# The second and third norm of a transformer step: rows scaled and transposed in place of a product with a diagonal, and half a unit started early

## The reference

```python
def rms_norm(x, w):
    xf = x.astype(jnp.float32)
    y = xf * lax.rsqrt(jnp.mean(xf * xf, axis=-1, keepdims=True) + NORM_EPS)
    return (y * w.astype(jnp.float32)).astype(x.dtype)

def modulate(h, shift, scale):
    return h * (1 + scale) + shift

def ffn_sublayer(x, shift, scale, gate, norm_w, wi, wo):
    return x + 0.5 * gate * swiglu(modulate(rms_norm(x, norm_w), shift, scale), wi, wo)

def mixer_inputs(x, shift, scale, norm_w, w_in):
    z = modulate(rms_norm(x, norm_w), shift, scale) @ w_in
    ...
```

## Time and profile before

| | us |
|---|---|
| median of three runs | 2199.97 (2198.9 to 2200.54) |
| the profiled execution | 2200.38 |
| its span, from first to last instruction | 2198.3 |
| TensorE busy in it | 2168.2 |
| VectorE busy | 1658.8 |
| ScalarE busy | 1077.2 |

### The profile page before, as it was taken

One profiled execution on the slowest core, in us unless ns is written; L12 is line 12 of the kernel. 1 busy time (PEld: TensorE's weight loads), 2 busy tenths in 40 slices (PEclk: granted clock), 3 DMA queues, 4 the chain that ended last, 5 costly groups with the idle time before them and its releaser, 6 DMA issues.

```text
span 2198.3 us, 28344 instructions
## 1 busy us (share of the span) xinstructions
PE 2168.2 (99%) x10272; PEld 1734.6 (79%) x10272; DVE 1658.8 (75%) x1903; ACT 1077.2 (49%) x1450; POOL 65.3 (3%) x55
## 2 busy tenths in 40 slices
PE   6999999999999999999999999999999999999999
PEld 3567777777777778888888888888888888888887
DVE  3447888888888889756867888885578686776856
ACT  3335444545435446455545545465554455555453
POOL 0001000000000000001600000100000000000000
PEclk9999999999999999999999999999999999999999
DMA  9998888888888876555536776845665757557573
GB/s 367 386 379 302 295 317 315 281 303 286 316 308 289 290 262 221 184 173 172 187 109 233 258 254 236 292 161 207 235 235 192 267 191 267 191 202 257 190 233 131
DMA packets 273333, 548.14 MB, mean 249 GB/s; under 512 B 9014, under 2 KB 9418, under 8 KB 273008
## 3 DMA queue, kind: packets, MB, share of 16 engines
q1 hardware_dynamic: 212676, 423.69, 55.7%
q10 hardware_dynamic: 57484, 113.47, 14.3%
q0 software_dynamic: 3104, 10.05, 1.6%
HBM read 543.71 MB, written 3.46 MB: 249 GB/s over the span
## 4 chain that ended last, share of the span: by engine, by line
PE 95%; DVE 2%; DMA 1%; ACT 1%; issue 0%; SPq 0%; ACTq 0%; DVEq 0%
PE ps L714 30%; PE ps L716 29%; PE ps L715 29%; PE ps L655 1%; PE ps L640 1%; DMA ada_w_sb<-in_ada_w 1%; DVE w_lo L1833 1%; PE ps L701 0%; PE ps L1091 0%; PE ps L1159 0%; PE ps L1167 0%; DVE xm L1953 0%; ACT w_hi L1342 0%; DVE vec_acc L1893 0%; DVE scan L2272 0%
## 5 line engine op out<-in xcount | busy, mean ns | idle before, releaser
L1342 ACT CAST w_hi<-raw_w 128x1024 fp32r<-128x1024 f32 x728 | 765.0, 1053 | 991.8 <-PE ps L716 942.5
L1833 DVE TENSOR_TENSOR w_lo<-raw_w,w_hi 128x1024 fp32r<-128x1024 f32 x728 | 896.4, 1235 | 384.7 <-ACT w_hi L1342 381.8
L714 PE MATMUL ps<-w_hi,xT_hi 128*128 128x512 f32 x2080 | 821.0, 395 | 5.5 <-DVE xT_lo L1921 4.2
L716 PE MATMUL ps<-w_hi,xT_lo 128*128 128x512 f32 x2080 | 810.7, 390 | 0.0
L715 PE MATMUL ps<-w_lo,xT_hi 128*128 128x512 f32 x2080 | 810.6, 390 | 0.0
L714 PEld LDWEIGHTS ps<-w_hi,xT_hi 128*128 128x128 f32 x2080 | 391.0, 188 | 110.2 <-issue 24.5
L716 PEld LDWEIGHTS ps<-w_hi,xT_lo 128*128 128x128 f32 x2080 | 390.8, 188 | 82.7
L715 PEld LDWEIGHTS ps<-w_lo,xT_hi 128*128 128x128 f32 x2080 | 391.0, 188 | 78.6
L1893 DVE SCALAR_TENSOR_TENSOR vec_acc<-ada_w_sb,ctile,vec_acc 128x512 f32<-128x512 f32 x420 | 299.2, 746 | 0.0
L714 PE MATMUL ps<-w_hi,hT_hi 128*128 128x512 f32 x704 | 275.8, 392 | 0.0
L716 PE MATMUL ps<-w_hi,hT_lo 128*128 128x512 f32 x704 | 274.1, 389 | 0.0
(11 more groups left out here) (287 smaller groups left out, 1059.2 us busy)
## 6 DMA issues: line engine op xcount, KB each, us to landing
raw_w<-in_ffn_wi SPq DMA_DIRECT2D x176, 1024.0 KB, 4.9
ada_w_sb<-in_ada_w ACTq DMA_DIRECT2D x96, 1024.0 KB, 8.0
raw_w<-in_ffn_wo SPq DMA_DIRECT2D x88, 1024.0 KB, 5.2
raw_w<-in_w_in SPq DMA_DIRECT2D x68, 1024.0 KB, 5.2
ada_w_sb<-in_ada_w SPq DMA_DIRECT2D x30, 1024.0 KB, 12.8
raw_w<-in_w_out SPq DMA_DIRECT2D x16, 1024.0 KB, 5.2
ada_m<-in_ada_w ACTq DMA_DIRECT2D x12, 1024.0 KB, 6.8
raw_w<-in_w_proj_m SPq DMA_DIRECT2D x8, 1024.0 KB, 5.1
```

What stands on the lines that cost most here:

```text
L714: pe.matmul(out, a_hi, w_hi[:, slot, kk, :], start=(first and kk == 0), stop=False)
L716: mm = pe.matmul(out, a_lo, w_hi[:, slot, kk, :], start=False, stop=(last and kk == 1))
L1342: act.copy(w_hi[:, us % SPL, :, :], raw_w[:, slot, 2 * half:2 * half + 2, :]).then_inc(hi_ready, 1)
L1833: dve.tensor_tensor(w_lo[:, us % SPL, :, :], raw_w[:, slot, 2 * half:2 * half + 2, :], w_hi[:, us % SPL, :, :].bitcast(F32), ALU.subtract) ...
```

## The change

In the second and third norm the diagonal goes. VectorE scales quarters 0 and 2 of a group's row by the inverse root and ScalarE quarters 1 and 3, into `acc` (second norm) or the new `rows_out` (third norm), and TensorE transposes the 16 blocks with the identity. The PSUM banks are laid out anew, four tiles to a bank. ScalarE now takes the even pairs and VectorE the odd ones. The context's part of pair 0 is cast and subtracted by itself, and TensorE runs the context's half of unit 0 ahead of the sample's transposes; the sample's half follows them. On VectorE the split of unit 1 moves ahead of the context's last two pairs, the half subtraction for the context stands ahead of the sample's inverse, and the splits of units 2 and 3 follow the subtractions of pairs 1 and 3. On ScalarE the splits ahead of the third norm are two in place of three; the third follows the cast of pair 1. For the second norm the sample's square of quarter 2 is taken after both context squares. The first norm keeps its diagonal.

```diff
-            def norm(s):
-
-                for g in range(GROUPS):
-                    pe.wait_ge(diag_ready, 2 * s + g + 1)
-                    for j in range(8):
...
-                        for b in range(2):
-                            k = 2 * j + b
-                            mm = pe.matmul(ps[:, j, b * TOK + g * P:b * TOK + (g + 1) * P],
-                                           x[:, g, k * P:(k + 1) * P], diag[:, g, :], start=True, stop=True)
-                        mm.then_inc(norm_ps, 1)
+            def norm_T(s, g, i):
+
+                pe.wait_ge(scaled_dve, 4 * (s - 1) + 2 * g + i // 2 + 1)
+                pe.wait_ge(scaled_act, 4 * (s - 1) + 2 * g + i // 2 + 1)
+                if g == LAT and i == 2:
+                    pe.wait_ge(xm_act, modulated(s, 2, CTX))
+                if g == LAT and i == 3:
+                    pe.wait_ge(xm_ready, modulated(s, 3, CTX))
+                for k in [2 * j + b for j in range(8) if norm_bank(j) == i for b in range(2)]:
+                    mm = pe.transpose(norm_tile(s, g, k), scaled_rows[s][:, g, k * P:(k + 1) * P], ident)
+                mm.then_inc(norm_ps, 1)
+
+            def norm_chunk(s, us):
+
+                for i in range(4):
+                    norm_T(s, CTX, i)
+                pe.wait_ge(xT_lo_ready, lows_before(s) + 1)
+                unit(us, 0, xT_hi, xT_lo, 0, 0, True, False, groups=(CTX,))
+                for i in range(4):
+                    norm_T(s, LAT, i)
+                for k in range(8):
+                    pe.wait_ge(xT_lo_ready, lows_before(s) + k + 2)
+                    unit(us + k, 0, xT_hi, xT_lo, 2 * k, 0, k == 0, k == 7, groups=(LAT,) if k == 0 else (CTX, LAT))
...
+            def scaled(s, g, n):
+
+                act.wait_ge(inverse_ready, 2 * s + g + 1)
+                c = slice(n * CH, (n + 1) * CH)
+                act.activation(scaled_rows[s][:, g, c], x[:, g, c], ACT.Copy, scale=small[:, 14 + g:15 + g]).then_inc(scaled_act, 1)
...
                 act.wait_ge(acol_ready, s + 4)
-                modulate(1, CTX)
+                modulate(0, CTX)
                 act.wait_ge(x_updated, s * NCH)
                 sumsq(s, 3, LAT)
+                hi(0, (CTX,))
                 root(s, LAT)
-                modulate(3, CTX)
-                modulate(5, CTX)
-                modulate(7, CTX)
-                modulate(1, LAT)
-                hi(0, 5)
-                hi(1, 5)
-                if s == 1:
-                    split(u0 + 2, 0)
-                modulate(3, LAT)
-                hi(2, 6)
-                hi(3, 6)
-                modulate(5, LAT)
-                hi(4, 7)
-                hi(5, 7)
+                modulate(2, CTX)
+                scaled(s, LAT, 1)
+                scaled(s, LAT, 3)
+                modulate(4, CTX)
+                modulate(6, CTX)
+                modulate(0, LAT)
+                hi(0, (LAT,))
+                hi(1)
+                split(u0 + 2, 0)
+                modulate(2, LAT)
+                hi(2)
+                hi(3)
                 split(u0 + AHEAD, 0)
-                modulate(7, LAT)
-                hi(6, 8)
-                hi(7, 8)
+                modulate(4, LAT)
+                hi(4)
+                hi(5)
+                modulate(6, LAT)
+                hi(6)
+                hi(7)
...
-                    for g in range(GROUPS):
-                        sumsq(1, 2, g)
+                    sumsq(1, 2, CTX)
                     act.wait_ge(x_ctx, 1)
                     sumsq(1, 3, CTX)
+                    sumsq(1, 2, LAT)
                     root(1, CTX)
+                    scaled(1, CTX, 1)
+                    scaled(1, CTX, 3)
                     split(U_IN + 1, 0)
...
-            for n in range(AHEAD):
-                split(U_F2 + n, 0)
+            split(U_F2, 0)
+            act.wait_ge(mac_done, VEC_F2)
+            scaled(2, CTX, 1)
+            scaled(2, CTX, 3)
+            split(U_F2 + 1, 0)
...
+            def scaled(s, g, n):
+
+                dve.wait_ge(inverse_ready, 2 * s + g + 1)
+                c = slice(n * CH, (n + 1) * CH)
+                dve.tensor_scalar(scaled_rows[s][:, g, c], x[:, g, c], small[:, 14 + g:15 + g], None, ALU.mult).then_inc(scaled_dve, 1)
...
                 dve.wait_ge(acol_ready, s + 4)
-                modulate(0, CTX)
+                modulate(1, CTX)
                 variance(s, LAT, 2 * NCH)
-                diagonal(s, LAT)
-                modulate(2, CTX)
-                modulate(4, CTX)
-                modulate(6, CTX)
-                modulate(0, LAT)
-                modulate(2, LAT)
-                lows(0, 1)
+                low_of(1, 0, (CTX,))
+                inverse(s, LAT)
+                scaled(s, LAT, 0)
+                scaled(s, LAT, 2)
+                modulate(3, CTX)
                 split(u0 + 1, 0)
-                modulate(4, LAT)
-                lows(2, 3)
+                modulate(5, CTX)
+                modulate(7, CTX)
+                modulate(1, LAT)
+                low_of(2, 0, (LAT,))
+                low_of(3, 1)
                 split(u0 + 2, 0)
-                modulate(6, LAT)
-                lows(4, 5)
+                modulate(3, LAT)
+                low_of(4, 2)
+                low_of(5, 3)
                 split(u0 + 3, 0)
-                lows(6, 7)
+                modulate(5, LAT)
+                low_of(6, 4)
+                low_of(7, 5)
+                modulate(7, LAT)
+                low_of(8, 6)
+                low_of(9, 7)
...
-                        variance(1, CTX, 2 * NCH - 1)
-                        diagonal(1, CTX)
+                        variance(1, CTX, 2 * NCH - 2)
+                        inverse(1, CTX)
+                        scaled(1, CTX, 0)
+                        scaled(1, CTX, 2)
...
             variance(2, CTX, 2 * NCH - 1)
-            diagonal(2, CTX)
+            inverse(2, CTX)
+            scaled(2, CTX, 0)
+            scaled(2, CTX, 2)
             split(U_F2, 0)
             dve.wait_ge(units_done, U_F2)
-            dve.tensor_tensor(y_tmp[:, LAT, :], ps[:, 3, :], gate_bc[:, LAT, c], ALU.mult).then_inc(y_read, 1)
-            dve.wait_ge(y_read, 1)
+            chain(dve.tensor_tensor(y_tmp[:, LAT, :], ps[:, 3, :], gate_bc[:, LAT, c], ALU.mult))
             dve.tensor_tensor(x[:, LAT, c], x[:, LAT, c], y_tmp[:, LAT, :], ALU.add).then_inc(x_updated, 1)
```

More of the change, by code:

```diff
@@ L276, in build @@
         hcT_lo = place("hcT_lo", [P, KD, TOK], F32R)
+        rows_out = place("rows_out", [P, GROUPS, D], at=SCR)
+        top[0] = SCR + (W_AT - SCR) % 256 + 32768
         vec_o = place("vec_o", [P, GROUPS, CH])
@@ L719, in unit, with x_chunk @@
                 return mm
-            def x_chunk(us, ux, banks, between=None, stage=None):
+            def x_chunk(us, ux, banks, between=None):
                 for k in range(8):
[L724 to L727, removed]
                     unit(us + k, ux, xT_hi, xT_lo, 2 * k, banks, k == 0, k == 7)
@@ L737, in gate_T, with ffn @@
                 mm.then_inc(gate_rows_ps, 1)
-            def ffn(f, u0, stage):
+            def ffn(f, u0):
                 def ffn_in(i, us, ux, ada=False):
@@ L760, in ffn_in @@
                         pe.wait_ge(ada_cols_done, 2 * i + 4)
-                    x_chunk(us, ux, 0, g_between, stage if first else None)
+                    if first:
+                        norm_chunk(2, us)
+                    else:
+                        x_chunk(us, ux, 0, g_between)
                     if not first:
@@ L967, in _ @@
             ada_fold(1, 1)
[L968 to L973, removed]
+            ffn(0, U_F1)
+            norm_chunk(1, U_IN)
+            x_chunk(U_IN + 8, 0, 2)
             pe.wait_ge(wg_ready, 1)
@@ L1324, in _ @@
                     mm.then_inc(ctx_done, 1)
-            norm(2)
-            ffn(1, U_F2, 2)
+            ffn(1, U_F2)
         @blk.scalar
@@ L1420, in modulate, with hi @@
                     for b in range(2):
                         k = 2 * j + b
-                        ins = act.activation(xm[:, k, g * P:(g + 1) * P], ps[:, j, b * TOK + g * P:b * TOK + (g + 1) * P],
+                        ins = act.activation(xm[:, k, g * P:(g + 1) * P], norm_tile(s, g, k),
                                              ACT.Identity, scale=acol[:, k, g:g + 1], bias=adacols[:, sh * KD + k, g:g + 1])
                     ins.then_inc(xm_act, 1)
-                def hi(j, done):
-                    act.wait_ge(xm_act if j % 2 else xm_ready, base + done)
-                    act.copy(xT_hi[:, 2 * j:2 * j + 2, :], xm[:, 2 * j:2 * j + 2, :]).then_inc(xT_hi_ready, 1)
+                def hi(j, groups=(CTX, LAT)):
+                    act.wait_ge(xm_ready if j % 2 else xm_act, modulated(s, j, groups[-1]))
+                    t = slice(groups[0] * P, (groups[-1] + 1) * P)
+                    act.copy(xT_hi[:, 2 * j:2 * j + 2, t], xm[:, 2 * j:2 * j + 2, t]).then_inc(xT_hi_ready, 1)
@@ L1911, in diagonal @@
```

(9 more changed lines are left out.)

42 lines of the change are left out of this document (26 added, 16 removed).

## The result

The changed kernel takes 2203.88 us (median of 20 runs, 2202.44 to 2205.43), the kernel before 2200.32 beside it (20 runs, 2198.79 to 2201.22): a ratio of 1.0016, 95% interval 1.001 to 1.0022. It is 3.6 us slower; 2.8 were predicted (2202.8 against 2199.97). The profiled execution took 2204.7 us, its span is 2202.8.

The account below looks back on a forecast made before the run. TensorE was taken to bound the kernel, with VectorE late at unit 4 after the change. 1.72 + 1.13 = +2.85 us gave 2203.2 profiled, 2202.8 as median; the 8-in-10 range was 2198.0 to 2205.8.

Parts of the forecast that it names:

- What bounds: TensorE, busy 99% of the span; gaps of 8.04 and 7.68 us at norms 2 and 3 are its work, not waits.
- Scaling: Per group, two 128x512 products each on VectorE and ScalarE, ScalarE's at 0.71 us; norm 2's transposes begin near 843.97, against 844.07.
- the sum: Queues laid out at measured spacings for norms 2 and 3: unit 4 late by 1.72 and 1.13 us, together +2.85 us.
- the list of signs: Three TensorE pauses per norm, clock at full level; last output matmul to unit 4 20.9 us in norm 2, 20.0 in norm 3.
- The queues: VectorE waits 1.67 us for ScalarE in norm 2; unit 4's split comes late, TensorE 1.72 and 1.13 us late by norm.
- Rivals 1 and 2: Norms 2 and 3: VectorE not late at unit 4, 2198.5 us (chance 0.11); all TensorE saves lands, 2192.7 us (0.04).
- rival 1: Unit 4, both norms: without the 1.67 us of waits and with tighter spacing, 0.61 + 0.86 us stay won, 2198.5; chance 0.11.
- Rival 3, the clock: TensorE's pauses among the transposes: a clock fall in the first costs 0.9 to 1.8 us per norm, about 2205.5; chance 0.12.
- What is moved past: Behind norm 2, ScalarE's four ada_w loads start about 4 us later, hidden by unit 8's lead of some 10 us.
- What can be told apart: Whole kernel: a difference under 0.2% (4.4 us) can't be told from no change; chance of same 0.74.

Follow-up runs that it names:

- early split: Against the changed kernel, unit 4's split (ScalarE's copy and VectorE's subtraction) moved ahead of the sample's last modulated pair: 2200.33 us.
- narrower split: Against the changed kernel, VectorE's subtractions for units 2 and 3 cover 512 of 1024 columns, so the output differs: 2200.58 us.
- The new order: Against the changed kernel, same instructions with both queues reordered: VectorE splits unit 1 first, context pairs 4 to 7 wait for their units: 2196.39 us.

## Why the prediction was right, and where not

- *What bounds.* Right: 64 transposes with single records 0.109 apart, 1.91 us for sixteen, and what TensorE saves turns into pauses.
- *Scaling.* ScalarE's 0.71, taken between 0.62 and 1.0, is the measured one (1.34 for two, 0.63 apart). The start of the context's transposes in the second norm was mis-sized: 0.38 us behind the last output matmul in the sum, 0.82 in the trace. The sum let the variance start earlier by the square that it no longer waits for. In the trace it does not wait for a square at all, but stands behind VectorE's split of the first unit, and that split follows the context's x, which is written 0.6 us later against TensorE than before; why it is later is open. VectorE before (the last output matmul starts at 843.59), then after (844.11):

```profile
840.30 0.69 DVE L2085 SCALAR_TENSOR_TENSOR x<-acc,x 128x512 f32<-128x512 f32 x1
...
842.92 0.16 DVE L1906 TENSOR_REDUCE small<-small 128x1 f32<-128x4 f32 x1 [0.62 <-ACT sg L1383]
```

```profile
841.41 0.69 DVE L2146 SCALAR_TENSOR_TENSOR x<-acc,x 128x512 f32<-128x512 f32 x1
...
842.13 1.22 DVE L1875 TENSOR_TENSOR w_lo<-raw_w,w_hi 128x1024 fp32r<-128x1024 f32 x1
843.26 0.15 DVE L1948 TENSOR_REDUCE small<-small 128x1 f32<-128x4 f32 x1
```

The half unit starts 4.35 us behind the last output matmul, 4.02 in the sum, and that 0.3 us is still there at unit 4: 21.31, where the sum gives 19.28 + 1.72 = 21.00 (the list of signs has 20.9). In the third norm the scaling lies under the sample's matmuls, and unit 4 came at 20.07, in the sum 18.96 + 1.13 = 20.09.
- *The queues.* Right in mechanism and size: pauses of 1.59, 1.60 and 2.13 us (forecast 1.8, 1.8, 2.2), each ended by the VectorE instruction named, with VectorE waiting for ScalarE's casts in between: 1.2 us in all in the second norm and 1.3 in the third, 1.67 forecast. An early split, a narrower split and, in the second norm, the missing half unit each moved unit 4 as the queues say, within 0.2 us.
- *Rivals 1 and 2* are out: they needed a VectorE that keeps up. The new order is the case that rival 1 looked for, and it takes other queues, not tighter spacing.
- *Rival 3, the clock.* This step failed in its place. The fall was priced for the first pause and said to be swallowed in the second; the third pause, ahead of unit 4, was given no fall at all. It is the one with nothing behind it to swallow the loss, and the traces put 1.65 us on it. The rule of the Trainium skill (TensorE: Matmul & The Clock Gate, Part 4: PE-mode transpose) was weighed for the pauses among the transposes; the traces of the changed kernel show no fall there, and the falls that they do show stand behind four units of matmuls and a wait. Without the half unit only transposes and waits stand between the units' matmuls, for 8.3 to 9.6 us. There the clock fell in the third norm in both such traces, and in neither second norm; in the six norms with diagonal products in that place it never fell. Whether the transposes or the waits among them (2.1 to 2.9 us each, but for one of 1.0) brought those two falls is not shown.
- *What is moved past.* ScalarE's ada_w loads: hidden as claimed, the stretch behind the second norm is 206.28 us in both. But the lead is shorter than the prediction's 10 us: in the trace before, VectorE's split of unit 8 ends at 868.15 and unit 8 starts on TensorE at 873.75, 5.6 us later, and after the change it is 5.6 as well. The step left out lies 210 us further on: 1.06 us back at the keys.
- *What can be told apart.* The prediction took differences under 4.4 us for no change. The runs tell more: the interval is 0.06% (1.3 us) to either side, and the 3.6 us are clear of it.

In all, +2.85 us were forecast; +2.1 and +1.2 for the two norms, -1.06 at the keys and some +1.7 for the clock give +3.9, and the medians differ by 3.6. The two that were missed have opposite signs and leave 0.6 between them: that the forecast of the time came closer than its steps is luck.

## What to carry to other kernels

Work taken off the busiest engine pays only as far as the queues that feed it keep up. Before cutting, lay out those queues in order and look for the last item that a unit waits for: here 7 us less work on TensorE made the kernel 3.6 us slower, moving one split up took 3.9 us off that, and a new order of both queues 7.8. Put what is needed last in time last in each queue, and what the next unit needs ahead of it. Price a clock fall behind each pause by itself, above all behind the last one.

## What was not expected of the hardware

- The same wait of 1.8 to 2.1 us brought a fall of the granted clock to 0.50 for 3.4 us in one norm of each trace of the changed kernel and not in the other, and not the same one in both; the waits of 1.64 us and less brought none in the norms in any trace here. One of 2.79 us brought it before the wait was over, but two of 2.85 us brought none, so the length of a wait does not decide it alone; what else does is open.
- VectorE's split of 1.23 us took 3.23 beside GpSimd's products, and GpSimd's second product 3.14 instead of 2.41. In both traces shown the split ends 1.1 us after GpSimd's first product (1083.94 against 1082.85, 1084.84 against 1083.76), nearly as if it began only then. The Trainium skill (SBUF — State Buffer, Who interferes with whom) has it that a VectorE instruction with two SBUF inputs contends with a GpSimd instruction that reads SBUF, and that contention for the port pair that the two engines share is an exclusive lock. The traces agree to within 0.15 us: behind the lock the split would end 1.23 us after the product, and it ends 1.1 us after it.
